# The last expert pair by quarters and column blocks, the final norm's weights spread by TensorE, a first store of 512 columns

## The chip, the core and the metric

The kernel runs on one core of one Trainium2 chip. A core has five engines with programs of their own: TensorE (PE in the profile: matmuls; PEld is its loading of stationary operands), VectorE (DVE), ScalarE (ACT), GpSimd (POOL) and SyncE (SP, which here issues nearly all transfers). They wait for each other by semaphores. Data comes from device memory (HBM) by 16 DMA engines into the on-chip memory of 128 partitions; TensorE writes into eight PSUM banks of 128 partitions by 512 f32. The metric is device time in microseconds of one execution, smaller is better, as a median over runs.

## What is computed

One layer of a hybrid block over 256 tokens of 2048 channels, all in float32. Behind two token mixers and their merge stands the part that matters here, a mixture of experts and a last norm:

```python
def _rmsnorm(x, w):
    xf = x.astype(jnp.float32)
    y = xf * lax.rsqrt(jnp.mean(xf * xf, axis=-1, keepdims=True) + EPS)
    return (y * w.astype(jnp.float32)).astype(x.dtype)

    def expert_rows(args):
        xb, e = args
        return (jax.nn.silu(xb @ w1[e]) * (xb @ w3[e])) @ w2[e]

    x = x + (jax.nn.sigmoid(mix_a) * ya + jax.nn.sigmoid(mix_b) * yb) @ w_out
    x = x + _hier_moe(_rmsnorm(x, norm_ffn), w_rg, b_rg, w_re, b_re, w1, w3, w2)
    return x

    return _rmsnorm(x, norm_final)
```

There are 32 experts; each token goes to two of them. `w1` and `w3` are 2048 x 512 for each expert, `w2` is 512 x 2048: 12 MB of weights for an expert, all read once from HBM.

## The kernel before

**Stages.** The first 800 us or so are the mixers, the merge, the output projection and the routing. From there the experts are taken in 16 pairs (`PAIRS`), in order: `expert_pair` (from L2165) runs once for each pair on TensorE, with a counterpart of the same name on ScalarE and VectorE. The tokens of an expert fill up to 64 slots (`CAP`), so that the two experts of a pair stand side by side: the first uses columns 0 to 63 of the array, the second columns 64 to 127. A pair is worked thus: `xeT` holds the gathered tokens, transposed; 16 steps over k for `w1` into bank 0, 16 steps for `w3` into bank 1 (L2200; one step is a matmul for each of the two experts); tanh and products give `hid`; four transposes (L2211) and a copy (L1050) give `aT`; the down product with `w2` goes into banks 4 to 7, one for each block k of 512 output columns (`CB`); ScalarE evicts a bank scaled (`y_hi`, L1061, in the last pair L1085), VectorE makes the rest (`y_lo`, L1624), and TensorE spreads the rows back over the tokens with four matmuls (`comb`), whose result VectorE adds to the residual `x1` (L1631). In all pairs but the last the gather for the next pair and other matmuls stand in the gaps.

**Transfers.** SP issues each weight transfer as soon as its place is free. A pair has twelve pieces j of 2 MB (0 to 3 are `w1`, 4 to 7 `w3`, 8 to 11 `w2`; even j is the first expert, odd j the second) that go round a ring of eight slots, `ringM`. Each wait is on the count `slotM_free`, which TensorE raises by two when it is through a half of a matrix. So `w3` of the last pair takes the places of `w2` of the pair before, and `w2` of the last pair those of its own `w1`. Each two slots have an arrival semaphore (`slotM0` to `slotM3`); where a slot is filled in parts, later parts have their own.

**The last pair.** The first half of `w3` (j = 4, 5) comes as two transfers of 2 MB (L532), one for each expert, the second half in four of 1 MB (L563). `w2` comes in ten (L570): columns 0 to 1023 in two pieces of t (the four row tiles of `w2`), then columns 1024 to 2047 in three. On TensorE `last_down` runs four pieces: half, two steps of t, within them the two column blocks of the half, within them the two experts (L2156). After pieces 1, 2 and 3 stands `combine(0)`, `(1)`, `(2)`, and at the end `combine(3)` (L2142, L2143).

**The final norm.** SP loads `norm_final`, spread over 128 partitions (`nfin`, 1 MB, L574) behind the last `w2` piece. ScalarE squares each 512 columns of `x1` after their last addition and sums them along the row (L1075). VectorE adds the partial sums (L1660), GpSimd takes the power -0.5 (L777). GpSimd has meanwhile multiplied columns 0 to 1023 by `nfin` (L773), and ScalarE scales them by the row's factor (L1101, 1024 columns in one instruction); VectorE does columns 1024 to 2047 in one operation (L1663). m counts the two halves of 128 tokens. SP issues four stores of 512 KB (L578): m = 0 low columns, high, m = 1 low, high.

The order of ScalarE in the last pair is written out: evict 0, evict 1, squares (0,0) and (0,1), evict 2, squares (1,0), evict 3, squares (1,1), and the rest. That of VectorE too: low part 0, 1, additions 0 and 1, low part 2, 3, additions 2 and 3.

Of the kernel before, what the change touches and what calls it, by code (L numbers as in the profile page):

```python
# [13 lines left out]
P = 128  # L14
# [73 lines left out]


# [40 lines left out]
def build(nc, x, norm_mix, w_in, conv_a, a_log, dt_bias, a_norm, w_gk2, b_gk, b_norm, w_oa, w_ob, w_out,  # L130
# [14 lines left out]
    with ExitStack() as ctx:  # L145
# [179 lines left out]
        nfin, junk = ringM[0][:, 0:D], ringM[1]  # L325
# [109 lines left out]

        class Splitter:
# [34 lines left out]
        def _(sp):  # L471
# [78 lines left out]
            load_pair(PAIRS - 1, more_rounds * PAIRS + (PAIRS - 2), 1, 0, RING_M - 2)  # L550

            def last_slot(j, piece):

                slot = (PER_PAIR + j) % RING_M
                if piece == 0:
                    sp.wait_ge(sem("slotM_free"),
                               more_rounds * (PAIRS * PER_PAIR) + ((PAIRS - 1) * PER_PAIR + j + 1))
                return ringM[slot], f"slotM{slot // 2}"

            for piece in range(2):  # L560
                for e in range(2):
                    slot, name = last_slot(RING_M - 2 + e, piece)
                    sp.dma_start(slot[:, piece * D:(piece + 1) * D],  # L563
                                 w3_v[2 * (PAIRS - 1) + e, :, (2 + piece) * D:(3 + piece) * D])\
                        .then_inc(sem("part_in" if piece else name), 16)
            for half in range(2):
                for piece, (t0, t1) in enumerate(((0, 2), (2, 4)) if half == 0 else ((0, 2), (2, 3), (3, 4))):
                    for e in range(2):
                        slot, name = last_slot(RING_M + 2 * half + e, piece)
                        sp.dma_start(slot[:, t0 * HALF:t1 * HALF].rearrange("p (t n) -> p t n", t=t1 - t0),  # L570
                                     w2_h[2 * (PAIRS - 1) + e, :, t0:t1, half * HALF:(half + 1) * HALF])\
                            .then_inc(sem(f"w2_tail{half + piece - 1}" if piece else name), 16)
            sp.wait_ge(sem("slotM_free"), more_rounds * (PAIRS * PER_PAIR) + (PAIRS * PER_PAIR + RING_M - 4))
            sp.dma_start(nfin, norm_final.partition_broadcast(P)).then_inc(sem("nfin_in"), 16)  # L574
            for m in range(NM):
                for h, name in enumerate(("y_lo", "y_hi")):
                    wait(sp, (name, m + 1))
                    sp.dma_start(y_v[:, m, h * HALF:(h + 1) * HALF], x1[:, m, h * HALF:(h + 1) * HALF])\  # L578
                        .then_inc(sem("y_out"), 16)
            sp.wait_ge(sem("y_out"), 32 * NM)  # L580

        @block.gpsimd
        def _(pool):
# [184 lines left out]
            pool.wait_ge(sem("nfin_in"), 16)  # L768
# [12 lines left out]
        def _(act):  # L781
# [287 lines left out]
            last = more_rounds * PAIRS + (PAIRS - 1)  # L1069
            gate_and_transpose(last)  # L1070
# [8 lines left out]
            def evict(k):  # L1079

                if k % 2 == 0:
                    act.wait_ge(sem("down"), last * (NC - 1) + k // 2 + 1)
                else:
                    act.wait_ge(sem("slotM_free"), last * PER_PAIR + (RING_M + 8 + 2 * (k // 2 + 1)))
# [8 lines left out]
            squares(1, 0)  # L1093
            evict(3)
            squares(1, 1)
# [3 lines left out]
            for m in range(NM):  # L1099
                act.wait_ge(sem("pool_end"), 2 * NM + m + 1)  # L1100
                nc.scalar.activation(x1[:, m, 0:HALF], xn[:, m], ACT.Copy, scale=rstd2[:, m:m + 1])\  # L1101
# [3 lines left out]
        def _(dve):  # L1105
# [383 lines left out]
            for c in range(NC):  # L1489
                cs = slice(c * CB, (c + 1) * CB)  # L1490
                sp_.follow(CH_MERGE + BCH * (c + 1))
                for m in range(NM):
# [4 lines left out]
                    if c == 0 and m == 0:  # L1497
                        dve.wait_ge(sem("x_back"), 16 * NM)
# [168 lines left out]
        def _(pe):  # L1667
# [464 lines left out]
            def last_down(n, u, arrived):  # L2132

                def combine(k):

                    pe.wait_ge(sem("ylo"), n * NC + (k + 1))
                    for m in range(NM):
                        j = 2 * k + m
                        if j >= 4:
                            pe.wait_ge(sem("xadd"), n * 8 + (j + 5))  # L2140
# [141 lines left out]
```

## Time and profile before

| | us |
|---|---|
| median of 3 runs (1741.49 to 1742.78) | 1741.64 |
| the profiled execution, total | 1743.75 |
| its span, first to last instruction | 1741.7 |
| TensorE busy in it | 1675.6 (96%) |
| VectorE, ScalarE, GpSimd busy | 672.6, 423.6, 178.0 |
| mean granted clock of TensorE | 0.992 |

The bytes read from HBM are 534.42 MB, 308 GB/s over the span. The page cuts the span into 40 slices of 43.5 us each; its rows there are the busy share of each engine in tenths, the granted clock of TensorE and the share of the DMA engines. The matmuls are pipelined: one starts while the one before still runs, and their ends are modelled, so starts tell more than ends. Most of TensorE's busy time in the expert part is work, but the stream of weights runs beside it all the time, and which of the two a stretch hangs on is told by the waits in it.

### The profile page before, as it was taken

The page shows a single profiled execution, that of the slowest core. Times are in us where ns is not written, and L with a number is a line of the kernel's source. Part 1 is how long each engine was busy: PE and PEld are TensorE (multiplying, and loading weights), DVE is VectorE, ACT ScalarE, POOL GpSimd, SP SyncE. Part 2 cuts the span into 40 slices and gives each one's busy share as a digit, 9 for nine tenths or more (in the row PEclk, how much of TensorE's full clock was granted, in tenths as well). Part 3 has the DMA queues.
Part 4 walks back from the last instruction along what each step waited for, and adds up shares of the span by engine and source line. Part 5 has one row for each costly group of instructions (what it writes and reads, how often), then busy time and mean ns, then how long its engine had stood idle before and what let it go on. Part 6 is the DMA issues. An engine that isn't in the chain of part 4 may idle for free.

```text
span 1741.7 us, 23731 instructions
## 1 busy us (share of the span) xinstructions
PE 1675.6 (96%) x10116; PEld 1085.1 (62%) x10116; DVE 672.6 (39%) x778; ACT 423.6 (24%) x452; POOL 178.0 (10%) x249
## 2 busy tenths in 40 slices
PE   8999999999999999999999999989999999999996
PEld 7898989988878888886444444334443434443432
DVE  5366778646845546542212222122112211221222
ACT  6344445334534433432000000000000000000002
POOL 6000042410341000000100000000000000000001
PEclk9999999999999999999999999999999999999998
DMA  8455445444544555877999999999999999999996
GB/s 255 152 183 163 160 137 187 137 138 145 169 146 123 184 186 192 314 289 271 417 413 427 428 428 428 428 429 429 428 428 429 429 429 429 429 427 427 430 424 280
DMA packets 96071, 537.59 MB, mean 309 GB/s; under 512 B 5804, under 2 KB 5868, under 8 KB 70012
## 3 DMA queue, kind: packets, MB, share of 16 engines
q1 hardware_dynamic: 95408, 535.85, 77.7%
q0 software_dynamic: 592, 0.69, 0.4%
q8 instruction: 57, 0.93, 0.2%
q14 instruction: 14, 0.11, 0.0%
HBM read 534.42 MB, written 2.10 MB: 308 GB/s over the span
## 4 chain that ended last, share of the span: by engine, by line
PE 72%; DMA 23%; DVE 2%; ACT 1%; issue 1%; SPq 0%; POOL 0%; DVEq 0%; ACTq 0%; POOLq 0%
DMA arena<-in_w 22%; PE psum L2200 13%; PE psum L1688 9%; PE psum L2225 9%; PE psum L1690 9%; PE psum L1689 9%; PE psum L2115 4%; PE psum L1709 3%; PE psum L1710 3%; PE psum L1711 3%; PE psum L2242 1%; PE psum L2243 1%; PE psum L2156 1%; PE psum L1934 1%; DVE w_lo L1121 0%
## 5 line engine op out<-in xcount | busy, mean ns | idle before, releaser
L2200 PE MATMUL psum<-arena 128*64 128x512 f32 x2048 | 457.1, 603 | 39.3 <-DMA arena<-in_w 38.4
L2200 PEld LDWEIGHTS psum<-arena 128*64 128x64 f32 x2048 | 147.7, 139 | 337.7 <-issue 286.9
L1121 DVE TENSOR_TENSOR w_lo<-arena,w_hi 128x2048 fp32r<-128x2048 f32 x119 | 276.1, 2325 | 179.6 <-ACT w_hi L787 179.3
L787 ACT ACTIVATE w_hi<-arena 128x2048 fp32r<-128x2048 f32 x119 | 227.5, 1914 | 265.1 <-PE psum L1690 172.9
L1688 PE MATMUL psum<-w_hi,hT_hi 128*128 128x512 f32 x568 | 226.9, 400 | 0.2 <-DVE w_lo L1121 0.2
L1690 PE MATMUL psum<-w_hi,hT_lo 128*128 128x512 f32 x568 | 224.3, 395 | 0.0
L1689 PE MATMUL psum<-w_lo,hT_hi 128*128 128x512 f32 x568 | 224.1, 395 | 0.0
L2225 PE MATMUL psum<-arena 128*64 128x512 f32 x960 | 210.8, 594 | 3.9 <-DMA arena<-in_w 3.9
L2225 PEld LDWEIGHTS psum<-arena 128*64 128x64 f32 x960 | 66.9, 137 | 136.5 <-issue 124.6
L1709 PE MATMUL psum<-hT_hi,w_hi 128*128 128x256 f32 x512 | 145.2, 284 | 0.0
L1710 PE MATMUL psum<-hT_lo,w_hi 128*128 128x256 f32 x512 | 143.2, 280 | 0.0
L1711 PE MATMUL psum<-hT_hi,w_lo 128*128 128x256 f32 x512 | 143.0, 279 | 0.0
L2115 PEld LDWEIGHTS psum<-arena 128*128 128x128 f32 x1024 | 120.3, 192 | 26.7 <-issue 25.2
L2115 PE MATMUL psum<-arena 128*128 128x128 f32 x1024 | 129.1, 279 | 0.1
L1624 DVE SCALAR_TENSOR_TENSOR y_lo<-psum,arena,y_hi 128x512 fp32r<-128x512 f32 x64 | 48.1, 751 | 194.1 <-ACT y_hi L1061 175.7
L1688 PEld LDWEIGHTS psum<-w_hi,hT_hi 128*128 128x128 f32 x568 | 106.6, 188 | 25.6 <-issue 0.6
L1690 PEld LDWEIGHTS psum<-w_hi,hT_lo 128*128 128x128 f32 x568 | 106.6, 188 | 24.6
L1689 PEld LDWEIGHTS psum<-w_lo,hT_hi 128*128 128x128 f32 x568 | 106.6, 188 | 24.4
L1616 DVE TENSOR_TENSOR arena<-arena,psum 128x512 f32<-128x512 f32 x16 | 11.0, 688 | 251.2 <-PE psum L2200 251.2
L1709 PEld LDWEIGHTS psum<-hT_hi,w_hi 128*128 128x128 f32 x512 | 96.8, 189 | 1.1 <-issue 0.3
L1710 PEld LDWEIGHTS psum<-hT_lo,w_hi 128*128 128x128 f32 x512 | 96.1, 188 | 0.1
L1711 PEld LDWEIGHTS psum<-hT_hi,w_lo 128*128 128x128 f32 x512 | 96.0, 188 | 0.0
(403 smaller groups left out, 1451.9 us busy)
## 6 DMA issues: line engine op xcount, KB each, us to landing
arena<-in_w SPq DMA_DIRECT2D x186, 2048.0 KB, 26.2
arena<-in_w_in SPq DMA_DIRECT2D x87, 1024.0 KB, 5.0
arena<-in_w_out SPq DMA_DIRECT2D x16, 1024.0 KB, 5.3
arena<-in_w SPq DMA_DIRECT2D x10, 1024.0 KB, 23.8
arena<-in_w_oa SPq DMA_DIRECT2D x8, 1024.0 KB, 5.1
arena<-in_w_ob SPq DMA_DIRECT2D x8, 1024.0 KB, 5.1
arena<-in_x SPq DMA_DIRECT2D x4, 1024.0 KB, 7.3
arena<-in_w SPq DMA_DIRECT2D x4, 512.0 KB, 15.3
```

The lines of the kernel that those rows point to most:

```text
L787: nc.scalar.activation(w_hi[x % NSPLIT], ringA[:, x % RING_A, :], ACT.Copy).then_inc(sem("w_hi"), 1)
L1121: tt(w_lo[x % RING_A], ringA[:, x % RING_A, :], w_hi[x % NSPLIT].bitcast(F32), ALU.subtract)\
L1624: stt(y_lo[k], bank(4 + k), rt["gate"][:, u:u + 1], y_hi[k].bitcast(F32), ALU.mult, ALU.subtract).then_inc(sem("ylo"), 1)
L1688: mm(m_banks[m], lhs[0][:, k0 + k, ms], wh[:, cs], start=(start and k == 0), stop=False)
L1689: mm(m_banks[m], lhs[0][:, k0 + k, ms], wl[:, cs], start=False, stop=False)
L1690: i = mm(m_banks[m], lhs[1][:, k0 + k, ms], wh[:, cs], start=False, stop=(stop and k == CT - 1))
L1709: mm(o, wh[:, cs], hTh[:, h * CT + k, :], start=first, stop=False)
L1710: mm(o, wh[:, cs], hTl[:, h * CT + k, :], start=False, stop=False)
L1711: i = mm(o, wl[:, cs], hTh[:, h * CT + k, :], start=False, stop=last)
L2115: i = mm(bank(2 + b % 2)[:, k * P:(k + 1) * P], h2[:, m, 4 * b + k, :], sel[:, m * P:(m + 1) * P], start=(m == 0), stop=(m == NM - 1))
L2200: i = mm(bank(w)[e * CAP:(e + 1) * CAP, :], xeT[:, k, e * CAP:(e + 1) * CAP], rows, start=(k == 0), stop=(k == KT - 1))
L2225: i = mm(bank(4 + k)[e * CAP:(e + 1) * CAP, :], aT[:, t * P + e * CAP:t * P + (e + 1) * CAP], src[e][:, (t % 2) * D + k * CB:(t % 2) * D + ...
```

## The change

Four things are changed, all but the last point in the last pair and behind it.

1. *Gate by quarters.* `w3` of the last pair comes in eight transfers of 1 MB: quarter by quarter, first expert, second expert. TensorE waits before each quarter.
2. *Down by column blocks.* `w2` comes in 16 transfers and TensorE takes it in the order `LAST_DOWN`: block k = 0 whole, k = 1 in halves of t, k = 2 in halves, k = 3 in a half and two single steps. A row of such a transfer is 512 columns, 2 KB, where it was 4 KB. `combine(0)` stands after the first half of k = 2, `combine(1)` after the first half of k = 3, `combine(2)` and `(3)` at the end. ScalarE has both squares of block 1 ahead of `evict(3)`.
3. *The norm's weights.* ScalarE loads `norm_final` as one row of 8 KB into one partition once the last gather is done. Between `w1` and `w3` of the last pair, TensorE multiplies a column of ones by that row, 512 columns at a time, into banks 2 and 3, and ScalarE copies each result to `nfin`. The 1 MB transfer on SP goes.
4. *Stores.* ScalarE's first scaling is split in 512 columns and 512 columns, and there are five stores: m = 0 columns 0 to 511; m = 0 columns 1024 to 2047; m = 0 columns 512 to 1023; m = 1 low; m = 1 high.

Beside these, the reload of x for the residual has a semaphore for each m (`x_in0`, `x_in1`) in place of one.

```diff
+LAST_DOWN = ((0, 0, FT, None), (1, 0, 2, 0), (1, 2, FT, 1), (2, 0, 2, None), (2, 2, FT, 2), (3, 0, 2, 3), (3, 2, 3, 4),
+             (3, 3, FT, 5))
...
-        nfin, junk = ringM[0][:, 0:D], ringM[1]
+        nfin_row, nfin = arena[0:1, H1:H1 + D], arena[:, H1 + D:H1 + 2 * D]
+        junk = ringM[1]
...
-                        sp.dma_start(x1[:, m, :], x_v[:, m, :]).then_inc(sem("x_back"), 16)
+                        sp.dma_start(x1[:, m, :], x_v[:, m, :]).then_inc(sem(f"x_in{m}"), 16)
...
-            load_pair(PAIRS - 1, more_rounds * PAIRS + (PAIRS - 2), 1, 0, RING_M - 2)
+            load_pair(PAIRS - 1, more_rounds * PAIRS + (PAIRS - 2), 1, 0, 4)
...
-            for piece in range(2):
+            for q in range(4):
                 for e in range(2):
...
+                    slot, name = last_slot(4 + 2 * (q // 2) + e, q % 2 == 0)
+                    sp.dma_start(slot[:, (q % 2) * D:(q % 2 + 1) * D],
+                                 w3_v[2 * (PAIRS - 1) + e, :, q * D:(q + 1) * D])\
+                        .then_inc(sem((name, "gate_second", name, "part_in")[q]), 16)
+            for k, t0, t1, tail in LAST_DOWN:
+                for e in range(2):
+                    slot, name = last_slot(RING_M + 2 * (k // 2) + e, tail is None)
+                    sp.dma_start(slot.rearrange("p (t n) -> p t n", t=FT)[:, t0:t1, (k % 2) * CB:(k % 2 + 1) * CB],
+                                 w2_h[2 * (PAIRS - 1) + e, :, t0:t1, k * CB:(k + 1) * CB])\
+                        .then_inc(sem(name if tail is None else piece_in(tail)[0]), 16)
+            for m, c0, c1, name, count in ((0, 0, CB, "y_lo", 1), (0, HALF, D, "y_hi", 1), (0, CB, HALF, "y_lo", 2),
+                                           (1, 0, HALF, "y_lo", 3), (1, HALF, D, "y_hi", 2)):
+                wait(sp, (name, count))
+                sp.dma_start(y_v[:, m, c0:c1], x1[:, m, c0:c1]).then_inc(sem("y_out"), 16)
...
-            sp.dma_start(nfin, norm_final.partition_broadcast(P)).then_inc(sem("nfin_in"), 16)
...
+            act.wait_ge(sem("gath"), more_rounds * (PAIRS * 4) + (PAIRS * 4 + 4))
+            act.dma_start(nfin_row, norm_final.rearrange("(a n) -> a n", a=1)).then_inc(sem("nmix_in"), 16)
+            for k in range(NC):
+                act.wait_ge(sem("nfin_row"), k + 1)
+                nc.scalar.activation(nfin[:, k * CB:(k + 1) * CB], bank(2 + k % 2), ACT.Copy).then_inc(sem("nfin"), 1)
             gate_and_transpose(last)
...
             squares(1, 0)
+            squares(1, 1)
             evict(3)
-            squares(1, 1)
...
-            for m in range(NM):
+            for m, c0, c1 in ((0, 0, CB), (0, CB, HALF), (1, 0, HALF)):
                 act.wait_ge(sem("pool_end"), 2 * NM + m + 1)
-                nc.scalar.activation(x1[:, m, 0:HALF], xn[:, m], ACT.Copy, scale=rstd2[:, m:m + 1])\
+                nc.scalar.activation(x1[:, m, c0:c1], xn[:, m, c0:c1], ACT.Copy, scale=rstd2[:, m:m + 1])\
                     .then_inc(sem("y_lo"), 1)
...
+                for k, t0, t1, tail in LAST_DOWN:
+                    if tail is None:
+                        src = arrived(8 + 2 * (k // 2))
                     else:
+                        wait(pe, piece_in(tail))
+                    for t in range(t0, t1):
+                        for e in range(2):
+                            at = t * HALF + (k % 2) * CB
+                            i = mm(bank(4 + k)[e * CAP:(e + 1) * CAP, :],
+                                   aT[:, t * P + e * CAP:t * P + (e + 1) * CAP], src[e][:, at:at + CB],
+                                   start=(t == 0), stop=(t == FT - 1))
+                    if t1 == FT and k < NC - 1:
+                        i.then_inc(sem("down"), 1)
+                    if k >= 2 and t1 == 2:
+                        combine(k - 2)
+                i.then_inc(sem("slotM_free"), 4)
+                combine(2)
+                combine(3)
...
+                    if w and not more:
+                        wait(pe, ("nmix_in", 32))
+                        for k in range(NC):
+                            if k >= 2:
+                                wait(pe, ("nfin", k - 1))
+                            mm(bank(2 + k % 2), ones[0:1, :], nfin_row[:, k * CB:(k + 1) * CB], start=True,
+                               stop=True).then_inc(sem("nfin_row"), 1)
...
-                        elif w and q == 3 and not more:
-                            wait(pe, ("part_in", 48))
+                        elif w and not more:
+                            wait(pe, ("gate_second", 32) if q == 1 else ("part_in", 48))
```

## Rows read from the trace of the kernel before

**Rows 1.** The page: busy share of the DMA engines, in 40 slices, tenths.

```profile
DMA  8455445444544555877999999999999999999996
```

**Rows 2.** Chain of waits, last 50 us: start us, us, what.

```profile
1662.39 30.47 DMA arena<-in_w
...
1692.90 13.98 PE psum L2200 x64
...
1709.28 7.94 PE psum L2156 x28
...
1724.70 2.75 PE psum L2156 x12
```

**Rows 3.** Timeline of TensorE, last pair: start, us, engine, line, operation.

```profile
1676.92 13.95 PE L2200 MATMUL psum<-arena 128*64 128x512 f32 x64
1692.90 13.95 PE L2200 MATMUL psum<-arena 128*64 128x512 f32 x64 [2.02 <-DMA arena<-in_w]
```

**Rows 4.** Timelines of TensorE at 95 and 226 us: f32 matmuls of 256 columns.

```profile
95.86 1.99 PE L1800 MATMUL psum<-arena 16*128 16x256 f32 x8
97.78 0.38 PE L1709 MATMUL psum<-hT_hi,w_hi 128*128 128x256 f32 x1
...
226.62 0.59 PE L1860 MATMUL psum<-arena 128*128 128x256 f32 x2
227.05 0.59 PE L1858 MATMUL psum<-arena 128*128 128x256 f32 x2
```

**Rows 5.** Transfers of w3, last pair: us from issue to landing.

```profile
arena<-in_w SPq DMA_DIRECT2D x1, 2048.0 KB, 26.0
...
L563 SPq DMA_DIRECT2D arena<-in_w x4: 327/432/1502, 1669.6 to 1672.1; - x4
...
DMA to landing us min/median/max: 24.4/27.6/30.8
```

**Rows 6.** Table by stretch: PE, PEld, DVE, ACT, POOL busy, clock, DMA share, GB/s.

```profile
8.00:12.00 4.00, 2.09 (x17) 1.89 (x16) 1.36 (x3) 2.31 (x5) 3.93 (x6) 1.00 1.04 399
12.00:16.00 4.00, 3.12 (x14) 2.58 (x15) 4.00 (x8) 4.00 (x7) 3.63 (x9) 1.00 1.05 386
1684.00:1688.00 4.00, 4.00 (x22) 1.29 (x18) 0.00 (x0) 0.00 (x0) 0.00 (x0) 1.00 1.01 430
1709.00:1715.00 6.00, 5.72 (x20) 2.27 (x22) 0.00 (x0) 0.03 (x1) 0.00 (x0) 0.72 1.03 410
```

**Rows 7.** Two transfers of 8 KB at the start: queue, KB, us to landing.

```profile
arena<-in_norm_mix SPq DMA_DIRECT2D x1, 8.0 KB, 4.8
...
arena<-in_norm_ffn POOLq DMA_DIRECT2D x1, 8.0 KB, 4.4
```

**Rows 8.** Table by stretch, one microsecond of the down product.

```profile
1710.00:1711.00 1.00, 1.00 (x6) 0.41 (x4) 0.00 (x0) 0.00 (x0) 0.00 (x0) 0.50 1.06 422
```

**Rows 9.** Timeline of TensorE, the first combine.

```profile
1718.77 0.50 PE L2142 MATMUL psum<-y_hi,comb 128*128 128x512 f32 x1 [0.71 <-DVE y_lo L1624]
```

**Rows 10.** Timeline of the tail, all engines.

```profile
1725.85 5.00 POOL L773 TENSOR_TENSOR arena<-arena 128x512 f32<-128x512 f32 x4 [106.10 <-DMA arena<-in_norm_final]
...
1728.68 0.68 ACT L1085 ACTIVATE y_hi<-psum,arena 128x512 fp32r<-128x512 f32 x1
...
1730.06 2.47 DVE L1631 TENSOR_TENSOR arena<-arena,psum 128x512 f32<-128x512 f32 x4
...
1733.60 2.19 ACT L1101 ACTIVATE arena<-arena 128x1024 f32<-128x1024 f32 x2 [0.27 <-POOL arena L777]
...
1734.77 2.88 SPq L578 DMA_DIRECT2D out_y<-arena  x4
```

**Rows 11.** Stores, first and last: KB, us to landing.

```profile
out_y<-arena SPq DMA_DIRECT2D x1, 512.0 KB, 2.7
...
out_y<-arena SPq DMA_DIRECT2D x1, 512.0 KB, 4.8
```

**Rows 12.** Timeline of VectorE, first sums of the residual.

```profile
726.13 1.28 DVE L1499 TENSOR_TENSOR arena<-psum,arena 128x512 f32<-128x512 f32 x2
```

More of the change, by code:

```diff
@@ L1079, in evict @@
             def evict(k):
[L1081 to L1082 removed]
+                if k < NC - 1:
+                    act.wait_ge(sem("down"), last * (NC - 1) + k + 1)
                 else:
[L1084 removed]
+                    act.wait_ge(sem("slotM_free"), last * PER_PAIR + (RING_M + PER_PAIR))
                 nc.scalar.activation(y_hi[k], bank(4 + k), ACT.Copy, scale=rt["gate"][:, 1:2])\
@@ L2140, in combine @@
                             pe.wait_ge(sem("xadd"), n * 8 + (j + 5))
+                        elif j in (2, 3):
+                            wait(pe, ("nfin", NC))
                         ms = slice(m * P, (m + 1) * P)
@@ L2143, in combine @@
                         mm(bank(j % 4), comb[u][:, ms], y_lo[k], start=False, stop=True).then_inc(sem("cmb"), 1)
-                for piece in range(4):
-                    half, tp = divmod(piece, 2)
-                    if tp:
-                        wait(pe, (f"w2_tail{half}", 32))
-                    else:
-                        src = arrived(8 + 2 * half)
-                    for t in range(2):
-                        if piece == 3 and t:
-                            wait(pe, ("w2_tail2", 32))
-                        for k in range(2):
-                            for e in range(2):
-                                i = mm(bank(4 + 2 * half + k)[e * CAP:(e + 1) * CAP, :],
-                                       aT[:, (2 * tp + t) * P + e * CAP:(2 * tp + t) * P + (e + 1) * CAP],
-                                       src[e][:, tp * D + t * HALF + k * CB:tp * D + t * HALF + (k + 1) * CB],
-                                       start=(tp == 0 and t == 0), stop=(tp == 1 and t == 1))
-                            if tp == 1 and t == 1 and k == 0:
-                                i.then_inc(sem("down"), 1)
-                    if tp:
-                        i.then_inc(sem("slotM_free"), 2)
-                    if piece:
-                        combine(piece - 1)
-                combine(NC - 1)
+                for k, t0, t1, tail in LAST_DOWN:
+                    if tail is None:
+                        src = arrived(8 + 2 * (k // 2))
+                    else:
+                        wait(pe, piece_in(tail))
[12 more added lines that the diff above has]
+                combine(3)
             def expert_pair(n, it, u, more, first=False):
```

33 lines of the change are left out of this document (10 added, 23 removed).

## The prediction

> **What bounds the kernel now.** I read the page's slices first: from the 20th slice to the last but one the DMA engines are busy nine tenths or more [rows 1], so the whole expert part streams its weights, and nothing that the change does can move that stream except what it takes out of it or what it does after its end. The chain of waits comes next. It leaves the stream at 1692.9 us, where the last pair's second weight matrix (w3) has landed, and from there to the end it is TensorE and then the last vector work [rows 2]. So the question is about 49 us at the end: TensorE's work from 1692.90, and the tail behind it. The timeline of TensorE shows its three blocks: w1 of the last pair from 1676.92, 64 instructions in 13.95 us, then 2.02 us of idle time "for DMA", then w3 from 1692.90 in 13.95 us [rows 3], then the transposes and the down product from 1709.28 [rows 2]. A matmul of the program on a 64-column half of the array is two instructions here, 32 of them in 13.95 us: 0.43 us each.
>
> The profiled execution took 1743.75 us for a span of 1741.7; the median shown is 1741.64. I work out a difference on the profiled span and put it on the median.
>
> **Gate by quarters.** Before, each expert's w3 half (2 MB) is one transfer. The first expert's lands at 1661.96 + 26.0 = 1688.0 [rows 5], the second's at 1662.39 + 30.47 = 1692.86 [rows 2], and TensorE needs both. In quarters the first quarter of both experts has the place of that first transfer and is there at about 1688.0, before w1 is through (1690.87; that end is modelled and lies past the last issue, so I take 1690.5). The DMA wait of 2.02 us goes. What is late next: the quarters after it. A quarter of w3 takes TensorE 3.43 us; the last one lands at 1672.1 + 30.8 = 1702.9 [rows 5], unchanged in order, and I add 0.3 us because 4 MB more now go in 8 KB rows, which the stretch at 1709 (4 KB rows, 410 GB/s) and that at 1684 (430) bound [rows 6]. So w3 can't begin before 1703.2 - 10.3 = 1692.9 without a stall on the last quarter. That is the time at which it begins today: the quarters by themselves are worth at most a few tenths, since the stream is nearly as slow as TensorE here.
>
> **The norm row on TensorE.** The quarters make room for four matmuls of a one-row constant by the row, 512 columns each, ahead of w3. No row shows this form. The nearest are the f32 ones of 256 columns on 128 columns of the array: two instructions every 0.43 us with 128 rows (226.62 to 227.05), and 8 instructions in 97.78 - 95.86 = 1.92 us with 16 rows [rows 4]. So 0.215 to 0.24 us for 256 columns, rows of the array make no difference, and 512 columns in two instructions are 0.86 to 0.96 us; here no second expert runs beside it. Four are 3.5 us (I take the first row; up to 3.85). The third waits for ScalarE to copy the first result out (a copy of this size is 0.7 us by [rows 10]), which the second one covers: first result at about 1691.6, copied at 1692.2, third due at 1692.25. So no more than 0.2 us is added. Bounds: 0 if they hid in the wait wholly, 3.85 + 0.2 above. Taken: w3 starts at 1690.5 + 3.5 = 1694.05, that is **+1.15 us**. The quarters are needed then at 1694.05, 1697.5, 1700.9 and 1704.3, all landed. Behind the waits on ScalarE stands only its tanh of the w1 result, which VectorE needs by 1708: covered by 13 us.
>
> **The row's load.** ScalarE issues 8 KB once the last gather is done, that is at the latest as w1 starts, 1676.9 [rows 3]. TensorE wants it 13.6 us later. At the kernel's start 8 KB on SP's queue took 4.8 us and 8 KB on GpSimd's 4.4 [rows 7], beside transfers at 399 GB/s [rows 6]. Against this: w3's transfers on SP's queue need 24 to 31 us in this stage [rows 5], and no row shows a transfer from ScalarE's queue. I take 5 us, nothing on the path; the upper bound is a rival. The Trainium skill, "DMA: Bandwidth & Descriptors", "Queues, rings and completion order", says that SP and ScalarE each own a row of rings and that a DMA engine goes round the rows by packets; by it the row would not stand behind SP's megabytes. What it replaces, a 1 MB broadcast, was the stream's last transfer, used by nothing before the tail: worth nothing on the path.
>
> **Down by column blocks.** The same 32 matmuls, and the same two combines between them. Today the first combine waits 0.71 us for VectorE [rows 9], since the block that it needs ends right before it; afterwards 5.2 us of matmuls stand between. **-0.71 us**. The stretch from 1709.28 holds one more thing: the granted clock is 0.50 at 1710 to 1711 [rows 8] and 0.72 over 1709 to 1715 [rows 6], so about 1.7 us are lost to the lower level (1.2 GHz) after the idle gaps around the transposes. Those gaps stay, and I leave the loss in; bounds: it goes (-1.7), or a second such stretch appears at w3 (+1.7).
>
> The loads now have 2 KB rows. The stretches with such rows at the kernel's start show 386 and 399 GB/s [rows 6], against 410 with 4 KB. At 386 from 1703.2 the pieces (8.39 MB) land thus: k=0 at 1708.6 (needed 1710.4), k=1 at 1714.1 and 1719.5 with half of k=2 ahead of it at 1716.8; first half of k=3 at 1722.2 (needed 1723.6), its ends at 1723.6 and 1724.9 (needed 1726.4 and 1727.3). No stall, with 1.4 us to spare at the tightest; a stall begins below 7.34 MB / 20.4 us = 360 GB/s. The same page of the Trainium skill, "Specifications", has line rate from 512 B up; by it the last piece would land near 1722.7. The trace disagrees (386 to 399 against 430), and I go by the trace. Six more SP issues are hidden: SP only waits for room there.
>
> **The tail.** Block k=2 of the down product ends at 1727.45 today [rows 2], the two matmuls of k=3 behind it at 1728.3; afterwards 1728.3 + 1.15 - 0.71 = 1728.7. Today the evictions of k=2 and k=3 come together, the squares stand between, and the one of k=3 starts 0.40 us after that matmul (1728.68), the four last sums at +1.78 (1730.06) [rows 10]. Afterwards k=2 has long left and k=3's eviction starts at once; VectorE does low part and then the sums, from about +1.43: **-0.35 us**. Squares, sum, power and final scaling follow each other as now. The change moves one square ahead of the last eviction; its input is there 0.8 us before the matmuls end, and it just fits (cover gone: +0.1 to 0.6 us). The final products start at 1733.60 today; they move by +1.15 - 0.71 - 0.35 = +0.09. The first store waits today for 1024 columns, two instructions in 2.19 us, so 1.1 us; with 512 columns 0.55 [rows 10]. **-0.55 us** for its issue. Is that worth as much at the end? Stores issued from 1734.77 land 2.7 us later for the first and 4.8 for the last [rows 11]: 1737.5 to 1741.3 is 3.8 us for three times 512 KB, 1.27 each, 413 GB/s, so they run at the engines' rate from the first on. Then the whole gain reaches the end. GpSimd's four products, 5.00 us from 1725.85 [rows 10], start earlier and stay hidden.
>
> The split of the x loads' semaphore saves nothing: the two sums run together at 726.13 with no idle time before them [rows 12].
>
> Sum: +1.15 - 0.71 - 0.35 - 0.55 = **-0.46 us**: 1741.2 us.
>
> **The rivals.**
> 1. *The reserve is found* (clock, or cheap matmuls). If the low clock stretch is absent or the four matmuls hide in the wait, 1.2 to 1.7 us more are won, but then the stream is the limit: the first half of k=3 lands at 1722.2 at 386 GB/s or 1721.6 at 399, so no more than 1.4 to 2.0 us. That gives 1739.2 to 1739.8; take 1739.5. For it: the low stretch hangs on short gaps that move. Against: the gaps are the same.
> 2. *The row comes late* (slower). ScalarE's transfer stands behind SP's, as SP's own do: landing 28 us after 1676.9, so 1704.9, against 1690.5. TensorE and all behind it wait 14.4 us: 1755.6. It decides from a landing of over 13.6 us. For it: 24 to 31 us in this stage. Against: the 4.4 us of another queue.
> 3. *Starvation or clock at the start*. Rows of 2 KB run at 330 GB/s here: 7.34 MB take 22.2 us, 1.8 more than there is; or the one-row matmuls let the clock fall during w3, +1.7. Both give about 1743.
> 4. *It does not do what it says*: the quarters bring nothing and the row's cost stays, as above; this is in the forecast.
>
> **How the numbers follow.** Forecast 0.50, rival 1 0.26, rival 3 0.14, rival 2 0.07, other mishaps 0.03. A measurement of this kernel can tell about 0.2%, 3.5 us. The forecast, rivals 1 and 3 all lie within it, since the stream caps any gain at about 2.5 us: same 0.86. Slower is rival 2 and most of the rest: 0.09. Faster than 1738.2 needs the stream to be quicker than any of its rows: 0.05. The range runs from rival 1 with some tenths to rival 3 with the upper price of the matmuls: 1738.8 to 1743.5.
>
> **What would show it.** Right: w3 starts near 1694 behind four matmuls of 0.86 us; no idle time before the first combine; the last eviction starts within 0.1 us of the last down matmul; the first store is issued near 1734.3. Wrong: idle time "for DMA" before the norm matmuls (rival 2) or inside the down product (rival 3); a granted clock of 1.00 all through the down product (rival 1).

## The result

The changed kernel takes 1745.56 us in the median of 22 runs (1740.94 to 1747.99), the kernel before 1742.30 in as many runs beside it (1740.69 to 1744.97). The ratio is 1.0014, 95% interval 1.0008 to 1.002: slower by 1.4 to 3.5 us, where 0.46 us less had been forecast, and 2 us above the upper end of the range (1743.5). The range was put on the earlier median of the kernel before, 1741.64; moved with the 0.7 us by which that kernel is slower here, its upper end is still 1.4 us under the result.

### The profile page after: what moved, and what is told of

Same layout as the page of the kernel before. It is cut to its first block, busy times and chain, and to the rows that moved or that the text cites. A ratio compares the mean times of both kernels' runs of the same rounds, so it can differ in the third digit from the quotient of the medians.

```text
span 1745.1 us, 23763 instructions
## 1 busy us (share of the span) xinstructions
PE 1683.1 (96%) x10124; PEld 1087.1 (62%) x10124; DVE 672.6 (39%) x778; ACT 426.0 (24%) x457; POOL 178.4 (10%) x249
## 4 chain that ended last, share of the span: by engine, by line
PE 73%; DMA 21%; POOL 2%; DVE 2%; ACT 1%; issue 1%; SPq 0%; DVEq 0%; ACTq 0%; POOLq 0%
DMA arena<-in_w 21%; PE psum L2216 14%; PE psum L2241 10%; PE psum L1699 9%; PE psum L1701 9%; PE psum L1700 9%; PE psum L2126 4%; PE psum L1720 3%; PE psum L1721 3%; PE psum L1722 3%; PE psum L2258 1%; PE psum L2259 1%; PE psum L2166 1%; POOL arena L623 1%; PE psum L1945 1%
## 5 line engine op out<-in xcount | busy, mean ns | idle before, releaser
L2216 PE MATMUL psum<-arena 128*64 128x512 f32 x2048 | 461.8, 608 | 36.1 <-DMA arena<-in_w 35.4
L2216 PEld LDWEIGHTS psum<-arena 128*64 128x64 f32 x2048 | 148.9, 140 | 338.8 <-issue 291.6
```

The source lines that it names most:

```text
L2216: i = mm(bank(w)[e * CAP:(e + 1) * CAP, :], xeT[:, k, e * CAP:(e + 1) * CAP], rows, start=(k == 0), stop=(k == KT - 1))
```

## The profile after

From the page of the changed kernel (span; busy time; the DMA engines' busy share in 40 slices; the queue that is new):

```profile
span 1745.1 us, 23763 instructions
...
PE 1683.1 (96%) x10124; PEld 1087.1 (62%) x10124; DVE 672.6 (39%) x778; ACT 426.0 (24%) x457; POOL 178.4 (10%) x249
...
DMA  7454545444544655877999999999999999999996
...
q10 hardware_dynamic: 2, 0.01, 0.0%
```

TensorE is busy 7.5 us longer than before (1683.1 against 1675.6) though only eight instructions were added, and the DMA slices look as in [rows 1]. q10 is ScalarE's one transfer. The profiled execution took 1747.99 us, span 1745.1, the slowest of the 22; the two profiled executions lie 3.4 us apart in span. 1.5 us of that stand already at the last pair's w1 (it starts at 1678.41 here, 1676.92 in [rows 3]): 1.2 us of it come from before 800 us, where nothing was changed on the path. In what follows I therefore count from the first matmul of the last pair's w1.

The timeline of TensorE (start, us, line, operation; L2216 is the expert matmul, L2193 the norm row, L2227 the transposes, L2166 the down product, L2155 the first combine):

```profile
1678.41 13.96 PE L2216 MATMUL psum<-arena 128*64 128x512 f32 x64
1692.29 5.29 PE L2193 MATMUL psum<-arena 1*128 1x512 f32 x8
1697.51 15.80 PE L2216 MATMUL psum<-arena 128*64 128x512 f32 x64
1714.10 0.75 PE L2227 MATMUL psum<-arena 128*128 128x128 f32 x4 [0.79 <-DVE arena L1627]
1715.73 8.80 PE L2166 MATMUL psum<-arena 128*64 128x512 f32 x40 [0.88 <-ACT arena L1056]
1724.46 0.50 PE L2155 MATMUL psum<-y_hi,comb 128*128 128x512 f32 x1
```

This answers [rows 3], and the chain of waits [rows 2] is here:

```profile
1692.36 5.22 PE psum L2193 x8
1697.58 15.75 PE psum L2216 x64
```

The wait for w3's DMA is gone from both, and so is the 0.71 us of [rows 9] ahead of the combine at 1724.46. But the four matmuls of one row take 5.22 us, and w3 behind them 15.80 us for the same 64 instructions that took 13.95. The table by stretch says why (busy time and count of PE, PEld, DVE, ACT, POOL; then the granted clock, DMA share, GB/s):

```profile
1692.00:1694.00 2.00, 2.00 (x6) 0.66 (x4) 0.00 (x0) 0.55 (x1) 0.00 (x0) 1.00 1.03 430
1694.00:1696.00 2.00, 2.00 (x4) 0.90 (x4) 0.00 (x0) 0.73 (x3) 0.00 (x0) 0.61 0.99 410
1696.00:1698.00 2.00, 2.00 (x4) 0.30 (x5) 0.00 (x0) 0.89 (x2) 0.00 (x0) 0.50 1.03 430
1698.00:1700.00 2.00, 2.00 (x6) 0.47 (x4) 0.69 (x1) 0.70 (x2) 0.00 (x0) 0.50 1.00 403
1700.00:1702.00 2.00, 2.00 (x10) 0.63 (x8) 0.00 (x0) 0.00 (x0) 0.00 (x0) 0.68 1.00 396
...
1716.00:1720.00 4.00, 4.00 (x20) 1.56 (x18) 0.00 (x0) 0.58 (x1) 0.00 (x0) 1.00 1.05 387
```

Inside the norm matmuls, while TensorE is busy without a gap, the granted clock goes to 0.50 and stays there until about 1701.3. In the down product, where the kernel before has its low stretch [rows 8], it is 1.00. Last comes the tail (compare [rows 10]):

```profile
1732.30 0.69 ACT L1096 ACTIVATE y_hi<-psum,arena 128x512 fp32r<-128x512 f32 x1 [0.29 <-PE psum L2166]
...
1733.69 2.47 DVE L1642 TENSOR_TENSOR arena<-arena,psum 128x512 f32<-128x512 f32 x4
...
1737.24 2.38 ACT L1112 ACTIVATE arena<-arena 128x512 f32<-128x512 f32 x3 [0.27 <-POOL arena L783]
...
1737.99 3.01 SPq L585 DMA_DIRECT2D out_y<-arena  x5
```

The eviction starts at 1732.30, 0.04 us after the last down matmul's end (1730.32 + 1.94, a modelled end), the sums 1.43 us after that end, the final products at +4.98, the first store 0.75 us after them. DMA brings 386 to 388 GB/s with the 2 KB rows.

## The experiments

All are compared with the kernel before on the same chip. The table gives, from each profiled execution, the time from the first matmul of the last pair's w1 to the first one of w3, of the transposes and of the down product, from there to the issue of the first store, and where the granted clock was 0.50 in the last pair (differences of starts in the timelines). Medians are of the timed runs.

| kernel | w3 | transposes | down | down to store | low clock | median | before beside it |
|---|---|---|---|---|---|---|---|
| before | 15.98 | 30.73 | 32.36 | 25.49 | down | | |
| changed | 19.10 | 35.69 | 37.32 | 22.26 | row, w3 | 1745.56 | 1742.30 |
| e10 changed, again | 18.53 | 35.69 | 37.32 | 22.24 | row, w3 | 1745.20 | 1742.57 |
| e1 no row | at once | 29.80 | 31.42 | 24.33 | none | 1742.01 | 1742.23 |
| e2 128 rows | 17.61 | 32.35 | 33.98 | 23.93 | down | 1742.85 | 1742.23 |
| e3 row alone | 17.60 | 32.35 | 33.97 | 23.78 | none | 1746.61 | 1742.23 |
| e4 row, four pieces | 14.93 | 33.28 | 34.91 | 22.25 | none | 1743.07 | 1742.23 |
| e9 row, two pieces | 15.80 | 32.60 | 34.23 | 22.25 | none | 1742.89 | 1742.57 |
| e5 row twice | 22.44 | 39.03 | 40.66 | 22.25 | row, w3 | 1751.45 | 1741.99 |
| e6 quarters, stores | at once | 30.93 | 32.55 | 25.06 | down | 1742.12 | 1741.99 |
| e7 half in blocks | at once | 30.11 | 31.74 | 23.77 | none | 1741.42 | 1741.99 |
| e8 blocks alone | 14.96 | 30.08 | 31.71 | 24.81 | none | 1742.22 | 1741.99 |

My theory after the trace: the four one-row matmuls cost their own time, and in most executions they let TensorE's clock fall, which costs about as much again (A). The timed runs have no trace of the last pair, so how often the clock falls is read from their times: in the changed kernel 17 of 22 runs took 1744.0 us or more, in the kernel before 3 of 22. The rivals: the 2 KB rows and the new order of the down product lost the time (B); the clock fell by chance or for another reason, and rows don't matter (C).

**e1: no norm row on TensorE.** The three other parts stay.

```diff
-            act.wait_ge(sem("gath"), more_rounds * (PAIRS * 4) + (PAIRS * 4 + 4))
-            act.dma_start(nfin_row, norm_final.rearrange("(a n) -> a n", a=1)).then_inc(sem("nmix_in"), 16)
...
+            sp.dma_start(nfin, norm_final.partition_broadcast(P)).then_inc(sem("nfin_in"), 16)
...
-                            mm(bank(2 + k % 2), ones[0:1, :], nfin_row[:, k * CB:(k + 1) * CB], start=True,
-                               stop=True).then_inc(sem("nfin_row"), 1)
```

> The changed kernel with the norm's weights taken back from TensorE: SP loads them spread over the partitions, 1 MB behind the last w2 piece, as before; quarters, column blocks, stores stay. Theory A (the one-row matmuls cost their own time and a stretch of low clock behind it): w3 starts within 0.1 us of w1's last matmul (0 to 2 us earlier than before relative to w1's start, so 13.9 to 14 us after it, against 19.1 in the changed kernel), low clock, if there is one, stands at the transposes or the down product; total 3 to 4 us below the changed kernel's typical 1745.6 and 0.5 to 2 us below the kernel before. Rival B (the column blocks with their 2 KB rows cost what was lost): the total stays at +2 to +3 us over the kernel before and TensorE waits for DMA inside w3 or the down product.

Ratio to before 1.0001 (0.9992 to 1.001). Against the changed kernel 3.55 us less by the medians, as A said, and no run of 1744.0 us or more in eleven. But the gain over the kernel before doesn't show, and TensorE does wait for DMA, which B had said. The timeline of TensorE (L2203 expert matmul, L2160 down product), and from that of the tail GpSimd's four products (L780) and the final products on ScalarE (L1108):

```profile
1676.84 24.25 PE L2203 MATMUL psum<-arena 128*64 128x512 f32 x112
1702.19 3.65 PE L2203 MATMUL psum<-arena 128*64 128x512 f32 x16 [1.10 <-DMA arena<-in_w]
1706.64 0.75 PE L2214 MATMUL psum<-arena 128*128 128x128 f32 x4 [0.79 <-DVE arena L1623]
1708.26 7.09 PE L2160 MATMUL psum<-arena 128*64 128x512 f32 x32 [0.88 <-ACT arena L1057]
1715.74 1.94 PE L2160 MATMUL psum<-arena 128*64 128x512 f32 x8 [0.39 <-DMA arena<-in_w]
...
1721.13 1.94 PE L2160 MATMUL psum<-arena 128*64 128x512 f32 x8 [0.46 <-DMA arena<-in_w]
...
1726.27 5.00 POOL L780 TENSOR_TENSOR arena<-arena 128x512 f32<-128x512 f32 x4 [106.67 <-DMA arena<-in_norm_final]
...
1731.84 2.37 ACT L1108 ACTIVATE arena<-arena 128x512 f32<-128x512 f32 x3 [1.06 <-POOL arena L784]
```

w3 follows w1 without a break for three quarters, waits 1.10 us for the last, and the down product waits 0.39 and 0.46 us more. From the down product to the first store it is 24.33 us here, 22.26 in the changed kernel, and this gain of the other parts went to two places. Up to the end of the last down matmul the waits cost 1.28 us (17.81 against 16.53). The other 0.79 us lie in the tail: the 1 MB of norm weights, again the stream's last transfer, landed only at 1726.1; GpSimd's four products behind it ran to 1731.27 and held up its power -0.5, and the final products began 5.77 us after the last down matmul instead of 4.98. So A holds for the loss, and B's mechanism for a part of where the gain went.

**e2: the same four matmuls with 128 rows.** The stationary operand has ones in row 0 and zeros below, so that the result is the same.

```diff
-                            mm(bank(2 + k % 2), ones[0:1, :], nfin_row[:, k * CB:(k + 1) * CB], start=True,
+                            mm(bank(2 + k % 2), ident[:, 0:1].to_broadcast([P, P]), arena[:, H1 + k * CB:H1 + (k + 1) * CB], start=True,
```

> The changed kernel, but the four norm matmuls use all 128 rows of the array (a stationary operand whose row 0 is ones and whose other rows are zero, the moving one is the row with 127 rows of other finite data under it); time of issue, columns and waits are the same. Theory A (a matmul of one row lets the granted clock fall): no low clock in or behind them, four matmuls in 3.5 us instead of 5.2, w3 in 13.95 instead of 15.8; w3 starts 17.4 us after w1; total 2 to 3.5 us less than the changed kernel, unless the low stretch comes back at the transposes (then 1 to 2 us less). Rival C (the clock falls for another reason, such as the gap before the third matmul or the length of the stretch, and rows do not matter): 5.2 and 15.8 us as in the changed kernel, same total.

Ratio 1.0003 (0.9994 to 1.0012), 2.7 us less than the changed kernel by the medians. Timeline and table by stretch:

```profile
1677.14 13.95 PE L2216 MATMUL psum<-arena 128*64 128x512 f32 x64
1691.02 3.80 PE L2193 MATMUL psum<-arena 128*128 128x512 f32 x8
1694.75 13.95 PE L2216 MATMUL psum<-arena 128*64 128x512 f32 x64
1709.49 0.75 PE L2227 MATMUL psum<-arena 128*128 128x128 f32 x4 [0.79 <-DVE arena L1627]
```

```profile
1692.00:1696.00 4.00, 4.00 (x13) 1.25 (x13) 0.03 (x1) 2.88 (x5) 0.00 (x0) 1.00 1.01 422
1696.00:1700.00 4.00, 4.00 (x22) 1.34 (x20) 0.66 (x1) 0.00 (x0) 0.00 (x0) 1.00 1.01 410
1712.00:1714.00 2.00, 2.00 (x7) 0.66 (x5) 0.00 (x0) 0.00 (x0) 0.00 (x0) 0.50 1.06 388
```

3.73 us for the four matmuls, 13.95 for w3, clock 1.00 through both. One profile alone would not decide against C, since four matmuls of one row can pass without a fall too (e3). The times do: 2 of 11 runs took 1744.0 us or more, like the kernel before. So rows matter, and C falls. This execution had its low stretch in the down product (0.50 at 1712 to 1714), as the kernel before has.

**e3: the norm row alone,** on the kernel before. The same three pieces of code as in the change's third point; w3, w2 and the stores as before.

```diff
+                    if w and not more:
+                        wait(pe, ("nmix_in", 32))
+                        for k in range(NC):
+                            if k >= 2:
+                                wait(pe, ("nfin", k - 1))
+                            mm(bank(2 + k % 2), ones[0:1, :], nfin_row[:, k * CB:(k + 1) * CB], start=True,
+                               stop=True).then_inc(sem("nfin_row"), 1)
...
-            sp.dma_start(nfin, norm_final.partition_broadcast(P)).then_inc(sem("nfin_in"), 16)
```

> The kernel before with the norm's weights by TensorE alone (one row load by ScalarE, four one-row matmuls between w1 and w3, no 1 MB load); w3 and w2 come and are worked as before, four stores. Theory A: the four matmuls start at once after w1, take 3.5 us of clock at full speed but 4.3 to 5.3 with the fall, w3 is slowed by up to 1.8 us behind them; since 2 us were idle there, the total is 1.5 to 4 us over the kernel before. Rival B (the cost lies in the column blocks): within 1.5 us of the kernel before.

Ratio 1.0025 (1.0015 to 1.0034), 4.4 us by the medians: the whole loss of the change and more comes with this part alone, and more than the 1.5 to 4 us expected. The executions stand in two groups: 1742.95 and 1743.05, and eight from 1745.08 to 1749.03. The profiled one is 1743.05, and there the clock didn't fall:

```profile
1690.39 3.79 PE L2190 MATMUL psum<-arena 1*128 1x512 f32 x8
1694.10 13.95 PE L2213 MATMUL psum<-arena 128*64 128x512 f32 x64
```

So 3.71 us (1694.10 - 1690.39) is the plain price of the four, and a row of the array or 128 of them make no difference to it. It also shows that four in one piece don't always bring the fall; what spared this execution stays open.

**e4 and e9: the one-row matmuls apart.** In the changed kernel, one ahead of each quarter of w3 (e4), or two ahead of the first and two ahead of the third (e9).

```diff
+                        if w and not more:
+                            if q == 0:
+                                wait(pe, ("nmix_in", 32))
+                            if q >= 2:
+                                wait(pe, ("nfin", q - 1))
+                            mm(bank(2 + q % 2), ones[0:1, :], nfin_row[:, q * CB:(q + 1) * CB], start=True,
+                               stop=True).then_inc(sem("nfin_row"), 1)
```

> The changed kernel with the four one-row matmuls spread: one ahead of each quarter of w3. The same work, but never more than 0.9 us of one-row matmuls at a time. Theory A: the clock stays at 1.00 through w3 (or falls for a part of the runs only), w1 start to w3 end is 13.9 + 3.5 + 13.95 = 31.3 us against 34.9 in the changed kernel; total 2 to 3 us below it. If what counts is the sum of one-row time and not its density, the low clock comes as before and the total is the same as the changed kernel's. Rival C: same as the changed kernel.

> The changed kernel with two of the one-row matmuls ahead of w3's first quarter and two ahead of its third: 1.9 us of one-row work at a time, where the changed kernel has 3.7 us in one piece and the fully spread version 1.05 us four times. Theory A (the share of one-row work in a stretch decides): falls in none or a few of the executions, median 1742.5 to 1744, w1's start to the transposes about 33.3 us in executions without a fall. Rival (any one-row matmuls of this sum bring the fall in most executions): median 1745 to 1746 with a gap between two levels.

e4: 1.0009 (1.0 to 1.0018); e9: 1.0003 (0.9994 to 1.0012). Both lie 2.3 to 2.5 us under the changed kernel, with the same one-row work, and 3 of 11 runs took 1744.0 us or more in each. The timelines, e4 and then e9 (L2208 and L2209 the norm row):

```profile
1690.89 1.12 PE L2208 MATMUL psum<-arena 1*128 1x512 f32 x2
1691.94 3.65 PE L2216 MATMUL psum<-arena 128*64 128x512 f32 x16
1695.53 1.12 PE L2208 MATMUL psum<-arena 1*128 1x512 f32 x2
```

```profile
1690.58 1.98 PE L2209 MATMUL psum<-arena 1*128 1x512 f32 x4
1692.49 7.09 PE L2217 MATMUL psum<-arena 128*64 128x512 f32 x32
```

No fall in either profiled execution; some of e9's timed ones (1744.4 to 1746.1, at a mean clock of 0.989 to 0.991) may have had one, which they don't show. What counts is that the four came in one piece. The parting has a price of its own: e4 pays 1.05 us for each where the four together took 3.71, and from w1 to the transposes it takes 33.28 us and e9 32.60, against 32.35 in e2 and e3, so some 0.3 us for each further piece. The expectation for e4, 31.3 us from w1 to the end of w3, had left that out; it took 32.5.

**e5: each one-row matmul twice,** in the changed kernel.

```diff
+                            mm(bank(2 + k % 2), ones[0:1, :], nfin_row[:, k * CB:(k + 1) * CB], start=True,
+                               stop=True)
```

> The changed kernel with each of the four one-row matmuls done twice (eight in all, the same result). Theory A (a stretch of one-row matmuls lets the granted clock fall, in most executions but not in all, since four of them take 3.7 us): 3.7 us more of plain cost, and now every execution falls, with the low stretch beginning inside the eight: no execution within 1743 us, median 1745.6 + 3.7 + 1 to 3 us = 1750 to 1752. Rival (the fall is a thing of chance in any stretch, the one-row matmuls only cost their time): median 1749 with the two levels of 1741 and 1745 moved up by 3.7, some executions still at 1745.

Ratio 1.0059 (1.0044 to 1.0075), median 1751.45, as A expected; four runs of 1748.27 to 1753.99, none at the lower level. Four runs are too few to say that the fall now always comes: with 5 in 22 spared, as in the changed kernel, four in a row would show none more often than one time in three. From the timeline of the eight:

```profile
1693.80 1.02 PE L2193 MATMUL psum<-arena 1*128 1x512 f32 x2
...
1695.52 1.66 PE L2193 MATMUL psum<-arena 1*128 1x512 f32 x2
1696.98 1.91 PE L2195 MATMUL psum<-arena 1*128 1x512 f32 x2
1698.82 15.80 PE L2218 MATMUL psum<-arena 128*64 128x512 f32 x64
```

The fall comes in the last two of the eight (1695.8 by the table by stretch), 5.5 us after the first and not at 2.2 as in the changed kernel; w3 again takes 15.80.

**e6, e8, e7: the other parts.** e6 is the kernel before with quarters and stores only, e8 with the column blocks only. e7 is e1 with the first half of w2 in 4 KB rows, two column blocks at a time:

```diff
-LAST_DOWN = ((0, 0, FT, None), (1, 0, 2, 0), (1, 2, FT, 1), (2, 0, 2, None), (2, 2, FT, 2), (3, 0, 2, 3), (3, 2, 3, 4),
-             (3, 3, FT, 5))
+LAST_DOWN = ((0, 2, 0, 2, None), (0, 2, 2, FT, 1), (2, 1, 0, 2, None), (2, 1, 2, FT, 2), (3, 1, 0, 2, 3), (3, 1, 2, 3, 4),
+             (3, 1, 3, FT, 5))
```

> The kernel before with the quarters of w3 and the five stores, but neither the row on TensorE nor the column blocks: w2 in 4 KB rows. Theory A': w3 starts at once after w1 and waits about 1.1 us for its last quarter, ends 0.3 to 0.9 us earlier after w1's start than before; the first store is issued 0.75 us after the final products start where it was 1.17; together 0.7 to 1.4 us under the kernel before. If stream-bound stretches eat it: within 0.3 us.

> The kernel before with the down product by column blocks alone (16 transfers of w2 with 2 KB rows, the new order on TensorE, one square moved ahead of the last eviction). Theory from the prediction: the 0.71 us wait ahead of the first combine goes, the final products start 4.97 us after the last down matmul where it was 5.32; at the same clock 0.7 to 1.1 us less from the start of the down product to that of the final products. Rival: waits for DMA inside the down product take it back, since 2 KB rows move at 387 GB/s: 0 to 0.4 us less.

> The version without the row on TensorE (quarters, column blocks, five stores, norm weights by SP), with the first half of w2 in two pieces of two column blocks each, rows of 4 KB, and only the second half by column blocks in 2 KB rows. Theory: the waits for DMA of 0.39 and 0.46 us inside its down product go or halve, since half of w2 moves at 410 instead of 387 GB/s; total 0.3 to 1 us under that version's 1742.0. Rival: the waits go elsewhere and the total is the same.

Ratios 1.0 (0.9991 to 1.0009), 1.0001 (0.9992 to 1.001) and 0.9999 (0.999 to 1.0008): none can be told from the kernel before. The waits of TensorE in e6, e8 and e7, in this order:

```profile
1697.78 3.65 PE L2199 MATMUL psum<-arena 128*64 128x512 f32 x16 [0.68 <-DMA arena<-in_w]
1702.75 3.65 PE L2199 MATMUL psum<-arena 128*64 128x512 f32 x16 [1.32 <-DMA arena<-in_w]
```

```profile
1715.82 1.94 PE L2161 MATMUL psum<-arena 128*64 128x512 f32 x8 [0.39 <-DMA arena<-in_w]
...
1721.21 1.94 PE L2161 MATMUL psum<-arena 128*64 128x512 f32 x8 [0.46 <-DMA arena<-in_w]
```

```profile
1704.10 3.65 PE L2204 MATMUL psum<-arena 128*64 128x512 f32 x16 [1.32 <-DMA arena<-in_w]
...
1714.34 5.37 PE L2161 MATMUL psum<-arena 128*64 128x512 f32 x24 [0.51 <-DMA arena<-in_w]
```

e6: what the quarters win at the start (w3 at once) they give back in waits of 0.68 and 1.32 us; the transposes start 30.93 us after w1, where it was 30.73, and the expectation that w3 would end earlier failed. e8: the wait ahead of the first combine is gone, but two waits for DMA stand in the down product, and it is 24.81 us to the first store where e3, in the old order and at the same clock, has 23.78. Of these 1.03 us, 0.5 come before the end of the last down matmul. The rest is the norm weights again: they land at 1726.2, and the final products start 5.83 us after that end, where the changed kernel, with the same order, has 4.98 (and e3, with the old one, 5.31). My expectation (0.7 to 1.1 us less) failed; its rival was nearer, and too mild still. e7 has shorter DMA waits in its down product than e1 (0.51 against 0.85 us), loses 0.80 us to the norm weights as e1 does, and has the shortest way from w1 to the first store, 55.51 us, with the lowest median; that it beats the kernel before, or e1, is not shown.

**e10: the changed kernel again.**

> The changed kernel itself, once more beside the others, to see its two levels again: most executions at 1744.3 to 1748 with a mean clock of 0.988 to 0.990, and about one in four at 1741 to 1742.2 with 0.992 or 0.993.

Ratio 1.0016 (1.0007 to 1.0025). From w1 to the transposes and from there on the stages are the same to 0.1 us; the fall came 0.5 us later after the first norm matmul, so that the four took 4.64 us and more of the loss lies in w3:

```profile
1690.56 4.71 PE L2193 MATMUL psum<-arena 1*128 1x512 f32 x8
1695.20 16.37 PE L2216 MATMUL psum<-arena 128*64 128x512 f32 x64
1712.36 0.75 PE L2227 MATMUL psum<-arena 128*128 128x128 f32 x4 [0.79 <-DVE arena L1627]
```

The two levels did not come back as clearly as expected: the runs spread from 1743.21 to 1747.96, 9 of 11 took 1744.0 us or more, and none lay at 1741 to 1742. In the first 22 the gap was plain: five of 1740.94 to 1742.15 us at a mean clock of 0.992 or 0.993, seventeen of 1744.28 and more at 0.988 to 0.990. The median of those five is 1741.68, 0.6 us under the kernel before, but they are picked by their time. That they had no fall is read from their mean clock, not seen.

## Why the prediction was wrong

*The row's load* was right. ScalarE issued it when w1 was about to start, and TensorE never waited for it:

```profile
1676.68 0.52 ACTq L1077 DMA_DIRECT2D arena<-in_norm_final  x1
```

The four matmuls began at 1692.29, with w1's last one, so it had landed within 15.6 us, while a transfer of 1 MB that SP issued in the same microsecond took 30.5; rival 2 is out. The Trainium skill, "DMA: Bandwidth & Descriptors", "Queues, rings and completion order", has the DMA engines go round the rows of SP and ScalarE by packets. The trace agrees: the row didn't stand behind SP's megabytes.

*The matmuls' plain price* was 0.2 us too low, 3.71 against 3.5, inside its bounds. A matmul costs the 0.86 us that was taken (1.72 us from start to start over two in e5, 1693.80 to 1695.52); what was missing is the change between the forms; and w1 takes 13.88 us to its last issue where I had taken 13.58. So w3 starts 1.62 us later than in the kernel before at full clock (17.60 in e3, 15.98), not 1.15.

*The clock* is the step that failed. The prediction had it as half of rival 3, "the one-row matmuls let the clock fall during w3, +1.7", and gave both halves together 0.14. By the times it comes in most executions, and it is twice the size: from w1 to the transposes the changed kernel takes 35.69 us, e2 and e3 with the clock at 1.00 take 32.35. That is 3.34 us, 1.5 us in the four matmuls (or 0.9 in e10) and the rest in w3. The stretch at half clock lasts 6.8 us, where the one from which 1.7 had been taken lasts 3.4 (0.72 over 6 us in [rows 6]). The sum's row for the matmuls [rows 4] gave a duration at full clock, from matmuls that stand singly among others, and I took the clock as something that idle time lowers, since [rows 8] come after idle gaps; why one-row matmuls lower it, these runs don't show. No row of before showed four one-row matmuls in one piece; the bound of this cost should have held a low stretch over the matmuls and w3.

*The other stretch of low clock,* the one in the down product, I kept in the sum for both kernels. It is a thing of the single execution: before, e2 and e6 show it in their profiles, e1, e3, e4, e7, e8 and e9 do not. The difference made on one profiled span of 1741.7 was then put on a median that is about 2 us under that execution. In the changed kernel's profiles the fall came earlier and the down product ran at 1.00, so the two profiles differ by less in the chain than the parts say. A clock of 1.00 all through the down product was the sign named for rival 1; it came true here without rival 1, because the fall had only moved.

*Down by column blocks and the tail* came out as worked out where the stream was ahead: from the down product to the first store 22.26 us, against 23.78 in e3 with the old order and the same clock. That is -1.52, forecast -0.71 - 0.35 - 0.55 = -1.61. The wait ahead of the combine went whole, the eviction started with the last matmul, the sums came 0.35 us sooner, the first store 0.42 rather than 0.55.

*That the store's gain reaches the end whole* was wrong: from its issue to the end of the span it is 7.11 us now and was 6.93 (1741.7 - 1734.77 [rows 10]). Of 0.42 us 0.24 are left; where the 0.18 us went, with five stores instead of four, isn't shown.

*No starvation* held, but for a reason I had not meant: 386 to 388 GB/s were measured where 386 was taken, and the pieces came in time because TensorE was late. The rule of the Trainium skill, "DMA: Bandwidth & Descriptors", "Specifications", line rate from 512 B up, is not borne out by 387 GB/s with 2 KB rows beside 430 with 16 KB. With the norm row taken away (e1) the down product starts 5.9 us earlier and runs into the stream.

*Rival 1,* cheap matmuls, named the stream as the limit and a gain of 1.4 to 2.0 us. e1 has the matmuls for nothing: its first store comes 55.75 us after w1, and the sum's own limit (1734.3 - 1.4 - 1676.9) gives 56.0. That they agree is half luck: the stream was 1.0 us ahead of the sum (the first half of k=3 begins 44.3 us after w1 and not 45.3), and the norm weights cost 0.79 us in the tail. The kernel before at full clock would need 32.36 + 23.78 = 56.14 (an estimate that puts e3's down product behind its own w3), so e1 had only 0.4 us to gain; most of rival 1's gain was the low stretch of one execution.

*The 1 MB transfer of the norm's weights* stood at nothing on the path. In the kernel before that is so: GpSimd's products end at 1730.85 [rows 10], and its power -0.5 waits for VectorE until 1732.99:

```profile
1732.99 1.17 POOL L777 TENSOR_TENSOR arena<-arena 128x1 f32<-128x1 f32 x2 [2.15 <-DVE arena L1660]
```

But with the shorter down product it becomes the limit, 0.79 us in e1, 0.80 in e7. So the row on TensorE bought something that the sum left out. By these rows e1 with its norm weights in time would be 1.2 us under the kernel before at full clock (56.14 - 54.96), an estimate; no run has this.

Put together for full clock: +1.62 - 0.71 - 0.35 - 0.24 = +0.3 us. The medians of e2 (+0.6) and e9 (+0.3) agree with it, but their intervals, -1.0 to +2.1 us, would hold a gain too. In the executions in which the clock falls it is 3.34 us more.

## What to carry to other kernels

When a gap on TensorE is filled with matmuls that use one row of the array, the price isn't only their duration: four in one piece brought the half clock in three of the four executions profiled with them (eight in a piece in e5) and, by the times, in most of the others, and slowed the full matmuls behind them, while the same four with 128 rows, or two and two, did not in the executions profiled. A gap "for DMA" beside a stream that is nearly as slow as the engine is worth next to nothing, because the engine meets the stream again a few microseconds later; ask where the last byte lands before costing the gap. That last byte can be one that nothing waited for until now, as the norm weights were: when the path in front of it gets shorter, cost it anew. And before a difference is built on one profiled execution, look at how far its time lies from the median and whether a low clock in it is there in others.

## What the runs showed of the hardware

- Half clock without idle time: TensorE was busy without a break when the granted clock fell to 0.50, 2.2 us (changed), 2.7 us (e10) and 5.5 us (e5) after the first one-row matmul. In all three it came back 6.8 us later, in the midst of full matmuls. e3's profiled execution had the same four matmuls and no fall. The starts and ends are worked out from the mean clock of the 2 us stretches, as in the tables above.
- Four 512-column f32 matmuls in one piece take the same with 1 row and with 128, 3.71 and 3.73 us at a granted clock of 1.00. Alone among full matmuls each costs 1.05 us (e4), in a row of its own kind 0.86 (e5).
- Loads with 2 KB rows move at 386 to 388 GB/s, with 4 KB rows at about 410, with 16 KB rows at 428 to 430.
